# In the two layers' attention, the two heads of a pair take turns in the matmuls of values and probabilities, key tile by key tile

## What is computed

```python
logits = jnp.einsum('bqhd,bqkd->bqhk', qb, kg).astype(jnp.float32) * attn_scale
logits = jnp.where(valid[:, :, None, :], logits, NEG_INF)
p = jax.nn.softmax(logits, axis=-1).astype(vg.dtype)
return jnp.einsum('bqhk,bqkd->bqhd', p, vg)      # the matmuls of the change
```

## Time and profile before

| what | value |
|---|---|
| median of 3 runs | 1308.26 us (1307.92 to 1308.77) |
| the profiled execution | 1305.94 us, of which the span is 1304.2 us |
| granted TensorE clock | 0.992 of full speed over the span |
| TensorE matmuls busy | 1268.6 us, 97% of the span |
| GpSimd busy | 985.0 us, 76% |
| ScalarE busy | 694.7 us, 53% |
| VectorE busy | 644.6 us, 49% |

### The profile page before, as it was taken

The page is one execution under the profiler, slowest core; times in us unless marked ns, Lnnn a source line. Parts: engine busy times, 40 slices in busy tenths (PEclk is TensorE's granted clock), DMA queues, the critical chain, the costliest instruction groups (busy, mean ns, idle before and its releaser), DMA issues.

```text
span 1304.2 us, 22550 instructions
## 1 busy us (share of the span) xinstructions
PE 1268.6 (97%) x9023; PEld 1160.8 (89%) x9023; DVE 644.6 (49%) x1477; ACT 694.7 (53%) x1276; POOL 985.0 (76%) x774
## 2 busy tenths in 40 slices
PE   6999999999999999999999999999999999999997
PEld 5988889998889888888999988989999988888886
DVE  5567646657565444411665477743025435444312
ACT  5454556455455766644544555665436545666532
POOL 4665658766559999988699666668888757899894
PEclk9999999999999999999899999999999999999999
DMA  6434335544345666655466444445666535566562
GB/s 237 139 120 130 116 113 177 162 131 150 105 134 177 186 191 189 193 178 184 139 185 192 160 130 132 132 142 159 181 180 211 175 102 157 185 189 191 178 193 81
DMA packets 57784, 208.92 MB, mean 160 GB/s; under 512 B 6352, under 2 KB 7632, under 8 KB 57424
## 3 DMA queue, kind: packets, MB, share of 16 engines
q1 hardware_dynamic: 57680, 207.48, 51.8%
HBM read 206.41 MB, written 1.05 MB: 159 GB/s over the span
## 4 chain that ended last, share of the span: by engine, by line
PE 90%; DVE 6%; ACT 2%; issue 1%; DMA 1%; SPq 0%; DVEq 0%
PE bank L348 19%; PE bank L352 17%; PE bank L354 16%; PE bank L353 16%; PE bank L350 9%; PE bank L832 2%; DVE xx L391 1%; PE bank L347 1%; PE bank L623 1%; PE bank L840 1%; PE bank L847 1%; ACT whi L307 1%; PE bank L2041 1%; DMA raw<-w_dram 1%; PE bank L2013 1%
## 5 line engine op out<-in xcount | busy, mean ns | idle before, releaser
L315 POOL TENSOR_TENSOR wlo<-raw,whi 128x512 fp32r<-128x512 f32 x770 | 984.8, 1307 | 303.9 <-ACT whi L307 303.0
L307 ACT ACTIVATE whi<-raw 128x1024 fp32r<-128x1024 f32 x387 | 403.3, 1052 | 25.2 <-PE bank L354 11.7
L352 PE MATMUL bank<-xx,whi 128*128 128x256 f32 (+1 forms) x1320 | 387.5, 294 | 12.6 <-DVE xx L391 10.4
L354 PE MATMUL bank<-xx,wlo 128*128 128x256 f32 (+1 forms) x1320 | 376.1, 285 | 0.0
L353 PE MATMUL bank<-xx,whi 128*128 128x256 f32 (+1 forms) x1320 | 376.0, 285 | 0.0
L352 PEld LDWEIGHTS bank<-xx,whi 128*128 128x128 f32 x1320 | 251.8, 191 | 21.9 <-issue 14.2
L353 PEld LDWEIGHTS bank<-xx,whi 128*128 128x128 f32 x1320 | 251.8, 191 | 0.5
L354 PEld LDWEIGHTS bank<-xx,wlo 128*128 128x128 f32 x1320 | 252.2, 191 | 0.0
L348 PE MATMUL bank<-xx,whi 128*128 128x512 f32 x704 | 240.3, 393 | 0.0
L350 PE MATMUL bank<-xx,wlo 128*128 128x256 f32 x616 | 172.9, 281 | 0.0
L348 PE MATMUL bank<-yy,whi 128*128 128x512 f32 x476 | 165.8, 397 | 0.0
(11 more groups left out here) (261 smaller groups left out, 1471.3 us busy)
## 6 DMA issues: line engine op xcount, KB each, us to landing
raw<-w_dram SPq DMA_DIRECT2D x387, 512.0 KB, 3.6
h<-x_dram SPq DMA_DIRECT2D x2, 544.0 KB, 6.1
cst<-con_dram SPq DMA_DIRECT2D x1, 1049.0 KB, 10.3
ar<-mem_dram SPq DMA_DIRECT2D x1, 1024.0 KB, 5.9
out_dram<-h SPq DMA_DIRECT2D x4, 256.0 KB, 2.5
cst<-con_dram SPq DMA_DIRECT2D x1, 134.0 KB, 3.6
prm<-par_dram SPq DMA_DIRECT2D x1, 131.0 KB, 3.5
```

The source lines that it names most:

```text
L307: e.activation(whi[:, i % NSPL, :], raw[:, i % NRAW, :], ACT.Copy).then_inc(*whi_done.done(i))
L315: return e.tensor_tensor(wlo[:, q, c0:c1], raw[:, i % NRAW, c0:c1], whi[:, q, c0:c1].bitcast(F), ALU.subtract)
L352: e.matmul(o, wh, both[:, 0, :], start=(i == 0), stop=False)
L354: m = e.matmul(o, wl, both[:, 0, :], start=False, stop=(i == len(feed) - 1))
```

## The change

The loop over key tiles becomes the outer one, and the two heads of the pair the inner one. TensorE waits once for the copy of the odd head's probabilities, ahead of both heads, where it waited for each head ahead of that head's matmuls. The completion event of each head stays on its last matmul. The number of matmuls and their operands stay the same.

```diff
         for s in range(8):
             if s == 4:
                 ob = side_.take(e, "ob", l, t)
-            for hh in (range(2 * s - 8, 2 * s - 6) if s >= 4 else ()):
-                pt, half = K.PT.at(l, t, hh), 64 * (hh % 2)
-                e.wait_ge(*s_out.of("pt", l, t, hh))
+            if s >= 4:
+                pair = (2 * s - 8, 2 * s - 7)
+                e.wait_ge(*s_out.of("pt", l, t, pair[1]))
                 for i, (vi, _, kn) in enumerate(kcs):
-                    m = e.matmul(ob[half:half + 64, 128 * (hh // 2):128 * (hh // 2) + 128], K.V[0:kn, vi, 0:64],
-                                 pt[0:kn, i, :], start=(i == 0), stop=(i == nn - 1))
-                m.then_inc(*piece.done("av", l, t, hh))
+                    for hh in pair:
+                        half = 64 * (hh % 2)
+                        m = e.matmul(ob[half:half + 64, 128 * (hh // 2):128 * (hh // 2) + 128], K.V[0:kn, vi, 0:64],
+                                     K.PT.at(l, t, hh)[0:kn, i, :], start=(i == 0), stop=(i == nn - 1),
+                                     skip_group_check=True)
+                        if i == nn - 1:
+                            m.then_inc(*piece.done("av", l, t, hh))
```

## The result

The changed kernel takes 1295.34 us (median of 5 runs, 1293.23 to 1298.6); the kernel before took 1308.26 us in the same rounds. The ratio is 0.9907, with a 95% interval of 0.9896 to 0.9918, so the change saves 12.2 us (10.7 to 13.6).

A forecast was written before the change was run, and what follows sets the result against it. TensorE was taken to bound the kernel. Savings of 5.6 us at `t` = 0 and 7.0 at `t` = 1, gross 12.6, less waits of 0.31 and 0.51, gave 1308.26 - 11.8 = 1296.5 us; range 1294.8 to 1300.

The forecast's parts named there:

- What bounds the kernel: Whole span: TensorE, busy 97%, bounds it; time taken from its program comes off the end unless another engine comes late.
- The two halves run at once: L832's pairs: the two heads' matmuls overlap in the array's two column halves, also with 16 rows.
- the mixer's 0.217 us for a pair: Mixer, 128-row matmuls alternating halves: one for each half takes 0.217 us together, so the second half is free.
- The price of a pair: L832's attention pairs: 0.74 us instead of 1.44 at `t` = 0, 1.01 instead of 1.87 or 1.88 at `t` = 1.
- the lag of the second half: In a longer run of positions the second half falls behind once, making the first position 0.42 us, 0.06 above 0.36.
- the lower bound: Pair at `t` = 1 if the second half has no lag at all: 0.94 us.
- The moved wait: First pair of layer 0: waiting for the odd head's copy ahead of the even head starts it 0.31 us later.
- The later chain in layer 1: Layer 1, second pair of `t` = 1: the odd copy doesn't move up with TensorE, which waits, losing 0.51 us.
- The sum: All 16 pairs: gross saving 12.6 us, less 0.31 and 0.51 us for waits, net 11.8 us.
- No overlap, no restart: L832's pairs: halves neither overlap nor restart; 1.16 us at `t` = 0, 1.60 at `t` = 1, time 1304.2 us; 5%.
- A change of half restarts the array: Pairs at `t` = 1: six restarts of 0.36, 2.16 us instead of 1.88; slower, 1310.8 us; 3%.
- The gain is given back at `t` = 1: Softmax chain late in all `t` = 1 steps, TensorE waits; only `t` = 0 pays, 5.6 - 0.3 us, time 1303.0; 6%.

The follow-up runs named there:

- the 128-row kernel head by head: The kernel before, its loop over heads and waits kept, with the meta keys' 16-row tile zero-padded to 128 rows: 1295.71 us, ratio to before 0.9902.
- the 128-row kernel with turns: The changed kernel with the meta keys' 16-row tile zero-padded to 128 rows: 1294.4 us, ratio to the kernel before 0.9897.

## Why the prediction was right

**What bounds the kernel.** Right: TensorE's 13.0 us came off the end, but for the two waits that I had looked for and two others.

**The two halves run at once.** Right: with both heads in one half the pairs took 1.16 and 1.59 us, and with two halves, in the same order, they take 0.73 and 0.95. The argument from the mixer's 0.217 us for a pair carried over, also to two heads that load the same values and to 16 rows. What the prediction left open is why the halves didn't run at once before. It is not the lack of turns as such: head by head with one row count, a pair at `t` = 0 takes 0.59 us too. The change from 128 back to 16 rows stood between the heads, and taking turns moved it away.

**The price of a pair.** 0.74 predicted at `t` = 0, 0.73 measured. At `t` = 1 the term was mis-sized: 1.01 predicted, 0.95 measured. I had added 0.06 us for the lag of the second half, taken from the mixer; here the second half stays 0.007 us behind to the end. The value lay near the lower bound that I gave (0.94). I had read the mixer's order as one by turns, but for its second tile two matmuls of a half stand together (L1679 and L1682), and the lag begins there: by the records the high half's loads start 0.007 us behind the low half's at first, then 0.11, and from there on 0.06. Why it does so there, and only by 0.013 us in the kernel that has 128-row tiles head by head behind the 16-row tiles, stays open. Gross saving 13.0 us, 12.6 predicted.

**The moved wait.** 0.31 predicted at the first pair, 0.4 measured, in the changed kernel and in the one that has this part alone. In the changed kernel the copy ends at 128.21 + 0.25 = 128.46, the first load starts at 128.57 and the first matmul at 128.60, 0.14 us after the copy where I had taken 0.05.

**The later chain in layer 1.** Right in place and about in size: 0.51 us predicted; ahead of the second pair at `t` = 1 TensorE is idle for 0.51 us for the copy of the odd head, and the pair starts 0.58 us later than without the wait (0.79 less 0.21).

**Two waits that I missed.** The first pair of layer 0 at `t` = 1 waits 0.26 us. I had listed it with 0.17 us to spare, and took it that the chain ahead of it keeps its length. It doesn't. One multiplication on VectorE (L917, now L921) takes 0.27 to 0.29 us mostly, but now and then far longer. Timeline of VectorE at that place, after:

```profile
147.34 0.28 DVE L911 SCALAR_TENSOR_TENSOR ar<-bank,ar 128x128 f32<-128x128 f32 x1
147.54 1.17 DVE L921 TENSOR_TENSOR yy<-ar,yy 128x128 fp32r<-128x128 f32 x1
148.64 0.28 DVE L911 SCALAR_TENSOR_TENSOR ar<-bank,ar 128x128 f32<-128x128 f32 x1
```

Before, a single one in the same group took 0.93 us; with the new phase it was 1.17, and another one took 0.38. From there to the pair VectorE waits only for ScalarE, and TensorE's own work is as long as before, so the chain arrives late. From the start of L1057 ahead of this group (145.93 us, before 149.80) to that of L902 at the pair (163.50 and 167.03) it is 17.57 us where it was 17.23, and the 0.34 more is about the size of the wait. Both times GpSimd ran its subtractions beside the long multiplication, which ended within 0.15 us after GpSimd's group did (148.57 us after, 151.70 before). Of the 32 multiplications of this line in the two kernels three ran beside GpSimd, and these are the three long ones. That GpSimd holds them up is argued from this, not tested apart. The other wait is for the transposes of layer 1's second pair at `t` = 0. They need probabilities that VectorE finishes at 322.69 + 0.50 = 323.19 us, and TensorE is through with the shorter pair at 323.08. I had checked the copies ahead of each pair, and the probabilities behind it only at `t` = 1. Together these two cost 0.65 us, against the 0.4 us by which I had priced the pairs too high.

**The sum.** 11.8 us predicted, 12.2 (10.7 to 13.6) measured by the ratio, and 11.1 and 11.3 in the two matched profiles once the clock's share is left out. That the 12.2 lies so close is in part luck: the pairs gave 0.4 us more than I had them at, and waits and small steps took 1.1 more.

**The rivals.** "No overlap, no restart" priced the pairs of the same-half kernel to 0.01 us, so it was the right price of another case. "A change of half restarts the array" fell with every kernel that has two halves. "The gain is given back at `t` = 1" held for 0.9 of 7.4 us. The Trainium skill's rule that I weighed (page "TensorE: Matmul & The Clock Gate", Part 3: loads overlap with matmuls in flight only if the row group differs) does not hold here: equal rows and different column halves overlap in all 40 pairs of matmuls of the changed kernel, and different row counts in different halves don't overlap where the 16-row tiles stand apart.

## What to carry to other kernels

Matmuls with 64 output partitions, as small as these (128 moving columns), should use both column halves by turns, and those that stand next to each other should have the same number of rows: the second half's matmul was free here, and a change of row count stopped both halves. Padding a 16-row operand with zero rows to 128 cost no array time and took such a stop away. When a stage on the bounding engine gets shorter, walk each of the next waits with the new start, the ones behind the stage as well as the ones ahead of it.

## What the runs showed of the hardware

- With float32 operands, 64 output partitions and 128 moving columns a matmul behind another of its shape adds 0.22 us, and behind one of another row count 0.36. In the other column half, with the same row count, it adds 0.01 or nothing.
- Matmuls don't start in program order across the two halves. The odd head's first load, told by the wait it carries, starts 0.014 us after the even head's, with one other matmul of the even head between them in the program; with two between them it starts 0.275 us after (the 128-row kernel head by head). Within a half no record shows a change of order.
- Executions of one kernel differ by up to 5 us (1293.23 to 1298.6 for the changed one), and the granted clock over the span goes with it: 0.994 in the shortest, 0.989 in the longest. In the profiles the difference sits in a few short stretches, where the projection matmuls of 272 columns take 0.43 us, at the 1.2 GHz level, and not 0.29, at 2.4: around 25, 95 and 620 us in the kernel before, each time behind waits of TensorE. In the profile of the 128-row kernel with turns one more came at 319 us, behind the wait of 1.4 us at L851 that the changed kernel has too, and cost 1.5 us, two thirds of what that kernel's pairs gain. For changes of 1 to 2 us the matched timelines tell more than the medians.
